# Down-weight sums moved two quads earlier, and the last activations stored in four pieces, in a macaron decoder layer in float32

## The chip, the cores and the metric

The kernel runs on one core of a Trainium2 chip. The time is device microseconds of one execution; the median of several runs is compared. The engines are named as in the profile: PE (TensorE), ACT (ScalarE), DVE (VectorE), POOL (GpSimd) and SP (SyncE, which here only issues DMAs and waits).

## The reference

```python
def swiglu(h, w_gu, w_down):
    g, u = jnp.split(h @ w_gu, 2, axis=-1)
    return (jax.nn.silu(g) * u) @ w_down
...
x = x + 0.5 * swiglu(rms_norm(x, ffn1_norm), ffn1_w_gu, ffn1_w_down)
h = rms_norm(x, mix_norm)
# q, k, v, u = split(h @ w_in): sliding-window attention beside causal pooling
x = x + concat([a, m]) @ w_out
x = x + 0.5 * swiglu(rms_norm(x, ffn2_norm), ffn2_w_gu, ffn2_w_down)
gate = sigmoid(rms_norm(x, ple_norm) @ ple_w_gate + ple_b_gate)
x = x + gate * rms_norm(p @ ple_w_proj, ple_post_norm)
```

Sequence 1024, model width 1024, hidden width 2816, all float32. The change touches the two `swiglu` calls only.

## The kernel before

Everything lies transposed (channels on partitions, tokens on the free axis). Each float32 factor is split into a high part (ACT rounds it to float32r) and a low part (DVE subtracts), and a product is three matmuls: high x high, low x high, high x low (helper `three`, lines 779 to 781). A matmul is 128 x 128 by 128 x 512.

Both matrix products of a feed-forward are computed as 2 x 2 blocks with seven block products instead of eight (P1, P2, Q3 to Q7), which needs sums and differences of the operands' blocks.

**Gate-and-up stage.** 22 quads, q = 0 to 21. A quad is one pair of hidden tiles; it loads 1 MB of weights (`quad_load`, into `raw[q % 2]`), DVE and ACT form and split its seven sums a quad ahead (`add_t`, `round_t`, `split_t`), and PE makes seven products of 12 matmuls each. DVE then gates the quad (`gated`), and behind every odd quad it forms the sums of the activations (`mix_acts`). SP stores these seven tiles of 128 x 512, 1792 KB, to DRAM as `actc[ph, j]`, j = 0 to 10 (`act_store`); the buffer `acts` is then free for the next pair.

**Down stage.** 77 steps: seven products in the order `ORDER2` = P1, P2, Q6, Q5, Q3, Q7, Q4, each over k = 0 to 10 (`FH` is 11). A step takes one tile `actc[ph, k][:, s, :]` and one block of down weights, both 256 KB, loads them into one of six ring slots (`ring_load`, `d_f`), ACT rounds the slot (`dn_hi`, line 1139), DVE subtracts (`dn_lo`, line 1620), and PE runs 12 matmuls on it. Slot i is loaded again when PE has done step i - 6. P1, P2 and Q3 read weights as given (`wd`), the others read sums of weights (`wdc`).

**The sums of the down weights** are made during the gate-and-up stage, in 22 chunks of 512 KB: SP loads a chunk into the single buffer `wdr` (`wd_load`, which waits until the chunk before is stored), POOL makes four additions in place (line 738), SP stores it (`wd_store`, which waits for POOL). They are first read by step 22.

**SP's order is written by hand** (`ffn` in the SP block), and every wait in it blocks all that stands behind. Turn q, from 1 to 21: in even turns the store of the activations of the pair before; load of chunk q - 1; its store; the gate-up load of quad q + 3 (waits for the split of quad q + 1). In turn 21 the ring loads of steps 0 to 3 stand ahead of chunk 20's load, and step 4's ring load ahead of its store. Then: load of chunk 21, ring load of step 5, store of chunk 21, ring load of step 6, store of the last activations (pair 10, one DMA of 1792 KB), ring load of step 7, and so on. From step 12 on each ring load is followed by a reload of a tile of x into memory that the activations used, so SP waits there once for all their stores.

`ph` is 0 for the first feed-forward and 1 for the second. ACT works strictly in program order too: behind step 12's rounding it copies the four P1 banks (`dp`), on which PE's step 11 and the rest of P2 depend.

Of the kernel before, what the change touches and what calls it, by code (L numbers as in the profile page):

```python
# [40 lines left out]
FH = FT // 2  # L41
# [32 lines left out]
P1, P2, Q6, Q7, Q5, Q4, Q3 = range(7)  # L74
# [5 lines left out]
QUADS = FT  # L80
# [13 lines left out]
RING = 6  # L94
STEP_INC = FH + 3

EARLY = 3
WD_AT = {P1: 0, P2: 2, Q3: 3}
WDC_AT = {Q5: 0, Q7: 1, Q4: 2, Q6: 3}
N_WD = 2 * FH  # L100

RES_FFN = 2 * KT
RES_MIX = 2 * KT
# [133 lines left out]
def program(nc, xT, pT, units, gu, wd, poolw, small, const, onehot, rel, band, e_dram, actc, wdc, x1, out):  # L237
    with ExitStack() as ctx:
# [7 lines left out]
        def place(name, shape, at, dt=F32):  # L246

            assert base <= at and at + size_of(shape) <= limit, (name, at, limit)
            return nc.alloc_sbuf_tensor_at(name, list(shape), dt, offset=at)
# [22 lines left out]
        def block_at(k, a):  # L272
            return r0 + 4 * KB * k + 2 * KB * a
# [5 lines left out]
        acts = place("acts", (P, 8, HALF), block_at(4, 0))  # L279
# [132 lines left out]
        def sem(name):  # L412
            return ctx.enter_context(nc.semaphore(name))
# [26 lines left out]
        gu_made, p1_copied, g0_made, g1_made = sem("gu_made"), sem("p1_copied"), sem("g0_made"), sem("g1_made")  # L440
        w2_made, w3_made, c22_made, c21_made, c12_made = (sem(n) for n in ("w2_made", "w3_made", "c22_made", "c21_made", "c12_made"))
        act_made, act_mixed, act_out = sem("act_made"), sem("act_mixed"), sem("act_out")
        wd_in, wd_made, wd_out = sem("wd_in"), sem("wd_made"), sem("wd_out")
        s2_in, t2_in = [sem(f"s2_in{i}") for i in range(RING)], [sem(f"t2_in{i}") for i in range(RING)]
        dn_rounded, dn_split, dn_made, dp_made = sem("dn_rounded"), sem("dn_split"), sem("dn_made"), sem("dp_made")
# [39 lines left out]
        def t_count(ph, n):  # L485

            return ph * (NGU - FIRST) + n + (1 if ph else 1 - FIRST)

        def t_ready(ph, n):
            return (t_pool, n + 1) if ph == 0 and n < FIRST else (t_split, t_count(ph, n))  # L490
# [7 lines left out]
        def step_done(ph, i):  # L498
            return dn_count(ph, i // FH, i % FH)
# [34 lines left out]
        def _(sp):  # L534
# [9 lines left out]
            def quad_load(ph, q):  # L544
                sp.dma_start(raw[q % 2][:, :], gu[ph, q]).then_inc(gu_in[q % 2], 16)

            def wd_load(ph, c):
                if c:
                    sp.wait_ge(wd_out, 16 * (ph * N_WD + c))
                else:  # L550
                    sp.wait_ge(s_made, (ph + 1) * N_MADE)
                sp.dma_start(wdr[:, :, 0:HALF], wd[ph, c // 2, c % 2].rearrange("p (i b) n -> p i (b n)", b=2)).then_inc(wd_in, 16)

            def wd_store(ph, c):
                sp.wait_ge(wd_made, 4 * (ph * N_WD + c + 1))
                sp.dma_start(wdc[ph, c // 2, c % 2].rearrange("p (i b) n -> p i (b n)", b=2), wdr[:, :, 0:HALF]).then_inc(wd_out, 16)

            def act_store(ph, j):
                sp.wait_ge(act_mixed, 4 * (ph * FH + j + 1))
                sp.dma_start(actc[ph, j], acts[:, 0:PRODUCTS, :]).then_inc(act_out, 16)  # L560

            def ring_load(ph, i):
                s, k, slot = ORDER2[i // FH], i % FH, i % RING
                if i >= RING:
                    sp.wait_ge(dn_made, step_done(ph, i - RING))
                elif i < 2:
                    sp.wait_ge(t_split, t_count(ph, GU_AT[(QUADS - 2 + i, Q3)]))
                else:
                    sp.wait_ge(gu_made, ph * NGU + NGU - 12 + 2 * (i - 1))
                if s == P1:  # L570
                    sp.wait_ge(act_out, 16 * (ph * FH + k + 1))
                elif s in WDC_AT:
                    sp.wait_ge(wd_out, 16 * (ph + 1) * N_WD)
                weights = wd[ph, k][:, :, WD_AT[s], :] if s in WD_AT else wdc[ph, k][:, :, WDC_AT[s], :]
                sp.dma_start(d_f[slot][:, 0:HALF], actc[ph, k][:, s, :]).then_inc(s2_in[slot], 16)
                sp.dma_start(d_f[slot][:, HALF:2 * HALF].rearrange("p (h n) -> p h n", h=2),
                             weights.rearrange("h p n -> p h n")).then_inc(t2_in[slot], 16)

            def x_reload(ph, n):
                a, k = n // KT, n % KT  # L580
                src = xT if ph == 0 else x1
                sp.dma_start(x_sb[:, k, tok(a)], src[k * P:(k + 1) * P, tok(a)]).then_inc(x_back[n // KH], 16)

            def ffn(ph, first_units):
                for q in (0, 1):
                    done, value = t_ready(ph, GU_AT[(q, Q3)])
                    sp.wait_ge(done, value)
                    quad_load(ph, q + 2)
                for q in range(1, QUADS):
                    if q == QUADS - 1:  # L590

                        for i in range(4):
                            ring_load(ph, i)
                    if q % 2 == 0:
                        act_store(ph, q // 2 - 1)
                    wd_load(ph, q - 1)
                    if q == QUADS - 1:
                        ring_load(ph, 4)
                    wd_store(ph, q - 1)
                    if q + 3 < QUADS:  # L600
                        sp.wait_ge(t_split, t_count(ph, GU_AT[(q + 1, Q3)]))
                        quad_load(ph, q + 3)
                wd_load(ph, N_WD - 1)
                ring_load(ph, 5)
                wd_store(ph, N_WD - 1)
                for i in range(RING, STEPS):
                    if i == RING + 1:
                        act_store(ph, FH - 1)
                    if i == FH + 1:
                        sp.wait_ge(wd_out, 16 * (ph + 1) * N_WD)  # L610
                        sp.wait_ge(act_out, 16 * (ph + 1) * FH)
                        sp.wait_ge(act_made, (ph + 1) * 2 * QUADS)
                    ring_load(ph, i)
                    if FH < i <= FH + 2 * KT:
                        x_reload(ph, i - FH - 1)
                    if i >= FH + 4 and (i - FH - 4) % 4 == 0 and first_units:
                        if len(first_units) >= SLOTS:
                            sp.wait_ge(gu_made, (ph + 1) * NGU)
                        unit_load(first_units.pop(0))
                    if i == 4 * FH:  # L620
                        sp.wait_ge(x_step, ph * XS + 3 * KH)
                        if ph == 0:
                            skewed = bass.AP(tensor=band.tensor, offset=P - 1,
                                             ap=[[SKEW - 1, P], [P * SKEW, N_Q_HEADS], [1, 2 * P]])
                            sp.wait_ge(band_out, 16 * N_Q_HEADS)
                            sp.dma_start(bias[:, :, :], skewed).then_inc(bias_in, 16)
                        else:
                            for j in range(4):
                                sp.wait_ge(e_out[j], 16 * (2 * KT // 4))
                            for a in (0, 1):  # L630
                                sp.wait_ge(re_out[a], 16)
                            sp.wait_ge(act_made, 4 * QUADS)
                            sp.dma_start(re_sb[0][:, :], e_dram[0, :, KT, :]).then_inc(re_in[0], 16)
                    if ph == 1 and 4 * FH < i <= 4 * FH + KT:
                        d = i - 4 * FH - 1
                        sp.dma_start(e_sb[0][:, d, :], e_dram[0, :, d, :]).then_inc(e_in[0], 16)
# [741 lines left out]
        def _(dve):  # L1378
# [131 lines left out]
            def gated(ph, q):  # L1510

                b, i, odd = ph * QUADS + q, q % 2, q % 2
                if not odd and b >= 2:
                    dve.wait_ge(act_out, 16 * (b // 2))
                dve.wait_ge(c12_made, b + 1)
                dve.wait_ge(g0_made, b + 1)
                dve.tensor_tensor(acts[:, (P1, P2)[odd], :], g0[i][:, :], w2[i][:, :], ALU.mult).then_inc(act_made, 1)
                dve.wait_ge(g1_made, b + 1)
                dve.tensor_tensor(acts[:, (A21, Q4)[odd], :], w3[i][:, :], c22[i][:, :], ALU.mult).then_inc(act_made, 1)
# [255 lines left out]
            for step in PLAN:  # L1775
# [16 lines left out]
                elif kind == "qks":  # L1792
                    a, what, i = step[1:]
                    j = QKS_AT[step[1:]]
# [5 lines left out]
                elif kind == "scores":  # L1800
# [3 lines left out]
                    for h in range(HPK):  # L1804

                        c = (h % 2) * 2 * P
# [6 lines left out]
                    c = C_SINK + kv * HPK  # L1813
# [14 lines left out]
                elif kind == "pv":  # L1828
                    u = step[1]
                    b, p0 = u // 2, (u % 2) * HEAD_DIM  # L1830
# [143 lines left out]
```

## Time and profile before

| | us |
|---|---|
| median of 3 timed runs | 1786.76 (1786.72 to 1788.21) |
| the profiled execution, whole | 1789.44 |
| its span, first to last instruction | 1787.3 |
| PE busy (matmul) | 1704.6, 95% |
| DVE busy | 1296.6, 73% |
| ACT busy | 697.2, 39% |
| POOL busy | 302.2, 17% |
| mean granted TensorE clock | 0.976 of full speed |

The mean rate of the DMAs over the span is 155 GB/s. The chain that ended last runs through PE for 72% of the span and DVE for 16%.

How to read the rows further down: a timeline row gives the start in microseconds from the start of the span, the duration, the engine, the line, the operation, what it writes and reads, how many instructions are merged in it, and in brackets how long the engine sat idle before it and what ended that. SPq rows are DMAs being issued; their duration is that of the issue. The first down stage begins (PE) at 507 us and the second at 1472 us.

### The profile page before, as it was taken

What the parts mean: (1) busy time and instruction counts of PE and PEld (TensorE: products, weight loads), DVE (VectorE), ACT (ScalarE), POOL (GpSimd) and SP (SyncE); (2) the same over time, 40 slices, a digit from 0 to 9 for tenths busy, and PEclk for the clock granted to TensorE, in tenths of its full rate; (3) what the DMA queues carried; (4) which work ended last, traced back from release to release, by engine and by line L of the source; (5) the groups of instructions that cost most, each with busy time, mean ns of one, the idle gap of its engine ahead of it and who ended that gap; (6) DMA issues with size and microseconds to landing.
All of it is one profiled execution on the core that took longest, in us unless ns stands there. A gap on an engine that the chain in (4) does not pass through costs nothing.

```text
span 1787.3 us, 20459 instructions
## 1 busy us (share of the span) xinstructions
PE 1704.6 (95%) x7314; PEld 1377.8 (77%) x7314; DVE 1296.6 (73%) x1812; ACT 697.2 (39%) x1120; POOL 302.2 (17%) x292
## 2 busy tenths in 40 slices
PE   7589999999999999999999889999999999999998
PEld 4368888888878887767677768888888887888877
DVE  7988677677655758678778699767767754676786
ACT  5343233232235444345645443322323323534442
POOL 5801222111220000024231001211122211000000
PEclk9789999999999999999899989999999999999999
DMA  7215444444469766121122313444444447876433
GB/s 283 75 49 212 153 165 148 159 166 158 139 232 312 218 212 199 48 71 48 36 77 81 114 71 120 175 159 154 170 155 164 147 151 269 289 235 204 153 117 125
DMA packets 124144, 277.69 MB, mean 155 GB/s; under 512 B 10219, under 2 KB 51852, under 8 KB 115468
## 3 DMA queue, kind: packets, MB, share of 16 engines
q1 hardware_dynamic: 116748, 263.02, 43.5%
q10 hardware_dynamic: 7296, 13.37, 2.1%
q8 instruction: 59, 0.97, 0.2%
q14 instruction: 41, 0.34, 0.1%
HBM read 198.23 MB, written 78.12 MB: 155 GB/s over the span
## 4 chain that ended last, share of the span: by engine, by line
PE 72%; DVE 16%; ACT 4%; DMA 3%; issue 3%; POOL 1%; SPq 1%; ACTq 0%; DVEq 0%; POOLq 0%
PE bank L779 23%; PE bank L780 23%; PE bank L781 23%; DVE qb L1796 1%; PE bank L1001 1%; DVE acc L1393 1%; DVE x_sb L1425 1%; DVE w_lo L1628 1%; DVE h_lo L1437 1%; DMA wdr<-in_wd 1%; DMA d_f<-in_wd 1%; ACT probs L1329 1%; DVE hn L1405 1%; DVE probs L1808 1%; POOL wdr L738 1%
## 5 line engine op out<-in xcount | busy, mean ns | idle before, releaser
L738 POOL TENSOR_TENSOR wdr<-wdr 128x256 f32<-128x256 f32 x176 | 172.1, 978 | 783.7 <-DMA wdr<-in_wd 773.4
L1620 DVE TENSOR_TENSOR dn_lo<-d_f,dn_hi 128x1024 fp32r<-128x1024 f32 x154 | 191.0, 1255 | 130.5 <-ACT dn_hi L1139 129.9
L779 PE MATMUL bank<-h_hi,t_hi 128*128 128x512 f32 x704 | 278.1, 395 | 6.4 <-DVE h_lo L1437 6.4
L780 PE MATMUL bank<-h_lo,t_hi 128*128 128x512 f32 x704 | 275.3, 391 | 0.0
L781 PE MATMUL bank<-h_hi,t_lo 128*128 128x512 f32 x704 | 275.2, 391 | 0.0
L779 PE MATMUL bank<-dn_hi 128*128 128x512 f32 x616 | 243.1, 395 | 9.4 <-DVE dn_lo L1620 9.4
L780 PE MATMUL bank<-dn_lo,dn_hi 128*128 128x512 f32 x616 | 241.8, 392 | 0.0
L781 PE MATMUL bank<-dn_hi,dn_lo 128*128 128x512 f32 x616 | 241.7, 392 | 0.0
L1139 ACT ACTIVATE dn_hi<-d_f 128x1024 fp32r<-128x1024 f32 x154 | 161.0, 1058 | 172.6 <-DMA d_f<-in_wd 102.9
L779 PE MATMUL bank<-c_hi,t_hi 128*128 128x512 f32 x528 | 205.5, 389 | 0.7 <-DVE c L1496 0.7
L781 PE MATMUL bank<-c_hi,t_lo 128*128 128x512 f32 x528 | 205.4, 389 | 0.0
L780 PE MATMUL bank<-c_lo,t_hi 128*128 128x512 f32 x528 | 205.4, 389 | 0.0
L779 PE MATMUL bank<-h_hi,w_hi 128*128 128x512 f32 x416 | 172.7, 415 | 7.4 <-ACT sig L1369 2.6
L780 PE MATMUL bank<-h_lo,w_hi 128*128 128x512 f32 x416 | 164.0, 394 | 0.0
L781 PE MATMUL bank<-h_hi,w_lo 128*128 128x512 f32 x416 | 163.6, 393 | 0.0
L779 PEld LDWEIGHTS bank<-h_hi,t_hi 128*128 128x128 f32 x704 | 133.3, 189 | 37.3 <-DVE h_lo L1437 5.2
L780 PEld LDWEIGHTS bank<-h_lo,t_hi 128*128 128x128 f32 x704 | 133.3, 189 | 28.8 <-issue 1.2
L781 PEld LDWEIGHTS bank<-h_hi,t_lo 128*128 128x128 f32 x704 | 133.0, 189 | 27.7
L1113 ACT ACTIVATE t_hi<-t_f 128x512 fp32r<-128x512 f32 x168 | 100.5, 624 | 126.4 <-DVE t_f L1457 119.1
L779 PEld LDWEIGHTS bank<-dn_hi 128*128 128x128 f32 x616 | 116.8, 190 | 37.2 <-DVE dn_lo L1620 12.3
L781 PEld LDWEIGHTS bank<-dn_hi,dn_lo 128*128 128x128 f32 x616 | 116.8, 190 | 24.6
L780 PEld LDWEIGHTS bank<-dn_lo,dn_hi 128*128 128x128 f32 x616 | 116.8, 190 | 24.5 <-issue 0.5
(165 smaller groups left out, 2607.0 us busy)
## 6 DMA issues: line engine op xcount, KB each, us to landing
raw<-in_gu SPq DMA_DIRECT2D x44, 1024.0 KB, 5.7
actc<-acts SPq DMA_DIRECT2D x22, 1792.0 KB, 6.7
d_f<-actc SPq DMA_DIRECT2D x154, 256.0 KB, 3.4
raw_m<-in_units SPq DMA_DIRECT2D x52, 512.0 KB, 4.1
wdr<-in_wd SPq DMA_DIRECT2D x44, 512.0 KB, 6.0
wdc<-wdr SPq DMA_DIRECT2D x44, 512.0 KB, 3.4
d_f<-wdc SPq DMA_DIRECT2D x88, 256.0 KB, 3.2
d_f<-in_wd SPq DMA_DIRECT2D x66, 256.0 KB, 4.7
```

The lines of the kernel that those rows point to most:

```text
L738: pool.tensor_tensor(blocks[to], blocks[one], blocks[two], ALU.add).then_inc(wd_made, 1)
L779: pe.matmul(ps, whi, vhi, start=first, stop=False, skip_group_check=onto)
L780: pe.matmul(ps, whi, vlo, start=False, stop=False, skip_group_check=onto)
L781: return pe.matmul(ps, wlo, vhi, start=False, stop=last, skip_group_check=onto)
L1001: last = pe.matmul(score_bank[h // 2][:, c + off:c + 2 * P], q_sb[p0:p0 + HEAD_DIM, h, b * P:(b + 1) * P], k_sb[p0:p0 + HEAD_DIM, max(b - ...
L1113: act.activation(t_hi[i][:, :], src, ACT.Copy).then_inc(t_rounded, 1)
L1139: act.activation(dn_hi[slot][:, :], d_f[slot][:, :], ACT.Copy).then_inc(dn_rounded, 1)
L1329: last = act.activation(probs[:, h, off:], probs[:, h, off:], ACT.Exp, bias=stats[:, NEGM, h:h + 1], accum_out=stats[:, DEN, h:h + 1])
L1393: dve.tensor_tensor(a, a, sq[i % 2][:, :], ALU.add).then_inc(squares_added, 1)
L1405: dve.scalar_tensor_tensor(hn[k % 2][:, :], x_sb[:, k, tok(nrm % 2)], col(g), rstd[nrm % 2][:, :], ALU.mult, ALU.mult).then_inc(h_normed, 1)
L1425: dve.scalar_tensor_tensor(x, x, col(C_GAIN[2 * ph] + k), rstd[a][:, :], ALU.mult, ALU.mult).then_inc(s_made, 1)
L1620: dve.tensor_tensor(dn_lo[slot][:, :], d_f[slot][:, :], plain(dn_hi[slot][:, :]), ALU.subtract).then_inc(dn_split, 1)
```

## The change

`WD_TURN` gives each of SP's turns its chunks: one a turn, but two in turns 6, 10 and 14, so that chunk 20 falls in turn 18, chunk 21 in turn 19, and none in turns 20 and 21. A chunk is now loaded and stored without anything in between (`wd_chunk`). The last activations are stored in four DMAs, `LAST` = slots 0, 1 to 2, 3 to 4 and 5 to 6 of the seven (256, 512, 512, 512 KB), each with a semaphore of its own, ahead of the ring loads of steps 7, 8, 9 and 10. A ring load with k = 10 waits for its piece. DVE's gating in the second feed-forward waits, in even quads, for all four pieces of the first.

```diff
+LAST = [(0, 1), (1, 3), (3, 5), (5, 7)]
...
+WD_TWO = (6, 10, 14)
+WD_TURN, _at = {}, 0
+for _q in range(1, QUADS):
+    _n = min(2 if _q in WD_TWO else 1, N_WD - _at)
+    WD_TURN[_q] = tuple(range(_at, _at + _n))
+    _at += _n
...
+            def last_store(ph, i):
+
+                lo, hi = LAST[i]
+                sp.wait_ge(act_mixed, 4 * (ph + 1) * FH)
+                sp.dma_start(actc[ph, FH - 1][:, lo:hi, :], acts[:, lo:hi, :]).then_inc(last_out[i], 16)
+
+            def wd_chunk(ph, c):
+                wd_load(ph, c)
+                wd_store(ph, c)
...
             def ring_load(ph, i):
...
-                if s == P1:
-                    sp.wait_ge(act_out, 16 * (ph * FH + k + 1))
-                elif s in WDC_AT:
+                if k == FH - 1:
+                    piece = [j for j, (lo, hi) in enumerate(LAST) if lo <= s < hi][0]
+                    sp.wait_ge(last_out[piece], 16 * (ph + 1))
+                elif s == P1:
+                    sp.wait_ge(act_out, 16 * (ph * (FH - 1) + k + 1))
+                if s in WDC_AT:
                     sp.wait_ge(wd_out, 16 * (ph + 1) * N_WD)
...
-                    wd_load(ph, q - 1)
+                    for c in WD_TURN.get(q, ()):
+                        wd_chunk(ph, c)
                     if q == QUADS - 1:
                         ring_load(ph, 4)
-                    wd_store(ph, q - 1)
...
-                wd_load(ph, N_WD - 1)
                 ring_load(ph, 5)
-                wd_store(ph, N_WD - 1)
                 for i in range(RING, STEPS):
-                    if i == RING + 1:
-                        act_store(ph, FH - 1)
+                    if RING + 1 <= i <= RING + len(LAST):
+                        last_store(ph, i - RING - 1)
                     if i == FH + 1:
                         sp.wait_ge(wd_out, 16 * (ph + 1) * N_WD)
-                        sp.wait_ge(act_out, 16 * (ph + 1) * FH)
+                        for j in range(len(LAST)):
+                            sp.wait_ge(last_out[j], 16 * (ph + 1))
...
                 if not odd and b >= 2:
-                    dve.wait_ge(act_out, 16 * (b // 2))
+                    dve.wait_ge(act_out, 16 * (b // 2 - ph))
+                    if ph:
+                        for j in range(len(LAST)):
+                            dve.wait_ge(last_out[j], 16)
```

## Rows read from the trace of the kernel before

**Rows 1.** Busy us of each engine (instructions) by stretch, granted clock, DMA share, GB/s.

```profile
510.00:540.00 30.00, 25.62 (x105) 20.40 (x104) 16.29 (x14) 8.49 (x8) 5.53 (x4) 0.94 0.73 254
...
1060.00:1440.00 380.00, 378.27 (x1656) 312.42 (x1655) 283.60 (x423) 121.21 (x213) 72.73 (x76) 0.99 0.43 152
1470.00:1500.00 30.00, 25.61 (x102) 20.35 (x101) 14.01 (x15) 8.44 (x9) 5.31 (x4) 0.92 0.68 241
```

**Rows 2.** PE's waits, 520 to 560 and 1480 to 1520: total us, times, longest.

```profile
PE bank L779 <- DVE dn_lo L1620: 4.4, 2, 3.6
...
PE bank L779 <- DVE dn_lo L1620: 4.4, 2, 2.6
```

**Rows 3.** Timeline of PE where both down stages begin.

```profile
518.29 0.39 PE L779 MATMUL bank<-dn_hi 128*128 128x512 f32 x1
...
521.01 0.39 PE L779 MATMUL bank<-dn_hi 128*128 128x512 f32 x1
...
531.29 0.50 PE L779 MATMUL bank<-dn_hi 128*128 128x512 f32 x1 [3.57 <-DVE dn_lo L1620]
...
533.05 0.63 PE L779 MATMUL bank<-dn_hi 128*128 128x512 f32 x1
...
538.49 0.39 PE L779 MATMUL bank<-dn_hi 128*128 128x512 f32 x1
...
1485.76 0.39 PE L779 MATMUL bank<-dn_hi 128*128 128x512 f32 x1
...
1504.84 0.39 PE L779 MATMUL bank<-dn_hi 128*128 128x512 f32 x1
```

**Rows 4.** Timeline of ACT in the first down stage: steps 6, 7, 9, 10.

```profile
522.32 1.06 ACT L1139 ACTIVATE dn_hi<-d_f 128x1024 fp32r<-128x1024 f32 x1 [9.12 <-DMA d_f<-in_wd]
528.92 1.06 ACT L1139 ACTIVATE dn_hi<-d_f 128x1024 fp32r<-128x1024 f32 x1 [5.53 <-DMA d_f<-in_wd]
...
532.59 1.06 ACT L1139 ACTIVATE dn_hi<-d_f 128x1024 fp32r<-128x1024 f32 x1 [0.36 <-DMA d_f<-in_wd]
534.02 1.06 ACT L1139 ACTIVATE dn_hi<-d_f 128x1024 fp32r<-128x1024 f32 x1 [0.37 <-DMA d_f<-in_wd]
```

**Rows 5.** Timeline of SP's queue around the start of the first down stage.

```profile
503.57 0.56 SPq L556 DMA_DIRECT2D wdc<-wdr  x1
506.66 0.58 SPq L552 DMA_DIRECT2D wdr<-in_wd  x1
...
517.34 0.55 SPq L575 DMA_DIRECT2D d_f<-actc  x1
...
518.82 0.55 SPq L560 DMA_DIRECT2D actc<-acts  x1
```

**Rows 6.** Timeline of DVE: the last pair of activations is mixed.

```profile
509.66 3.04 DVE L1528 TENSOR_TENSOR acts<-acts 128x512 f32<-128x512 f32 x4
```

**Rows 7.** DMA issues: count, KB each, median us from issue to landing.

```profile
raw<-in_gu SPq DMA_DIRECT2D x44, 1024.0 KB, 5.7
actc<-acts SPq DMA_DIRECT2D x22, 1792.0 KB, 6.7
```

**Rows 8.** Busy us by stretch, as in rows 1, while the old store runs.

```profile
520.00:525.00 5.00, 4.19 (x19) 3.18 (x18) 1.23 (x1) 1.06 (x1) 0.00 (x0) 1.00 1.10 413
```

**Rows 9.** Timeline of SP's queue in quads 6 and 7.

```profile
220.33 0.61 SPq L545 DMA_DIRECT2D raw<-in_gu  x1
223.10 0.57 SPq L552 DMA_DIRECT2D wdr<-in_wd  x1
231.87 0.54 SPq L556 DMA_DIRECT2D wdc<-wdr  x1
```

**Rows 10.** Timeline of ACT: first reading of quad 9's weights.

```profile
244.26 0.62 ACT L1113 ACTIVATE t_hi<-raw 128x512 fp32r<-128x512 f32 x1
```

**Rows 11.** Timeline of DVE: the sum and the gating of an even quad (8).

```profile
260.09 0.69 DVE L1508 TENSOR_TENSOR w<-bank,w 128x512 f32<-128x512 f32 x1 [2.03 <-PE bank L781]
260.87 0.69 DVE L1517 TENSOR_TENSOR acts<-g,w 128x512 f32<-128x512 f32 x1
```

More of the change, by code:

```diff
@@ L98 @@
 WD_AT = {P1: 0, P2: 2, Q3: 3}
+LAST = [(0, 1), (1, 3), (3, 5), (5, 7)]
 WDC_AT = {Q5: 0, Q7: 1, Q4: 2, Q6: 3}
 N_WD = 2 * FH
+WD_TWO = (6, 10, 14)
[4 more added lines that the diff above has]
+    _at += _n
+assert _at == N_WD
 RES_FFN = 2 * KT
@@ L442, in program @@
         act_made, act_mixed, act_out = sem("act_made"), sem("act_mixed"), sem("act_out")
+        last_out = [sem(f"last_out{i}") for i in range(len(LAST))]
         wd_in, wd_made, wd_out = sem("wd_in"), sem("wd_made"), sem("wd_out")
```

## Prediction

> **What bounds the kernel now.** I read the stretches first. They show TensorE (PE) busy for 378.27 of 380 us in the gate-and-up stage, but only 25.6 of 30 us where each of the two down stages begins, and there the granted clock falls to 0.94 and 0.92 [rows 1]. So PE is the bound, the gate-up stage has almost nothing left, and the holes lie at the two seams. The waits say what ended them: both times PE waited 4.4 us in two waits for dn_lo, VectorE's (DVE's) split of a ring slot [rows 2].
>
> The PE timeline sizes the holes. A step of the down stage is 12 matmuls, and takes 521.01 - 518.29 = 2.72 us. In the first down stage step 5 begins at 521.01 and step 9 at 538.49: four steps took 17.48 us where 10.88 is regular, so 6.60 us are lost. In the second they ran from 1485.76 to 1504.84, 19.08 us, so 8.20 us are lost [rows 3]. Together that is 14.80 us: 8.8 us of idle time [rows 2], and 6.0 us because PE runs at the lower clock level (1.2 GHz; matmuls of 0.63 us instead of 0.39) for some 8 matmuls behind a gap [rows 3]. From step 9 on a step is 2.72 us again.
>
> Then I asked who is late. PE waits for DVE, DVE for ScalarE (ACT), and ACT sat idle for 9.12 us ahead of step 6 and 5.53 us ahead of step 7 until the DMA into the ring slot landed [rows 4]. Why these DMAs were late stands in SP's queue [rows 5]. The slot of step 6 was free when PE ended step 0, at 521.01 - 4 x 2.72 = 510.13. But SP had the store of the second-last sums at 503.57, the last down-weight load at 506.66, and then had to wait until POOL had made the last sums and to store them; only then came the load of step 6, at 517.34, 7.2 us late. Behind it went the store of the last activations, 1792 KB in one DMA, at 518.82, and the load of step 7 was queued behind that: its slot had been free at 512.85, its data reached ACT at 528.92, 9 us after its issue. The second down stage has the same order of events.
>
> **The change, part by part.**
>
> Sums two quads sooner. The 22 chunks (load, four POOL adds, store) are all there still, but 20 and 21 move to quads 18 and 19, because quads 6, 10 and 14 take two. Between quad 20's activation store and step 6's load nothing of them is left. Step 6's load now follows its own gate at 510.2. With 4 to 5 us to land (my estimate from its old 517.34 to ACT at 522.32 [rows 4, 5]) and 2.4 us for ACT and DVE (528.92 for the ACT start, 531.29 for the PE start [rows 3, 4]) it is ready by about 517.6. PE wants it at 507.41 + 6 x 2.72 = 523.73: 6 us to spare. This takes away step 6's wait.
>
> The last activations in four pieces (256, 512, 512, 512 KB). The mix of the last pair ends at 509.66 + 3.04 = 512.70 [rows 6]. SP is then about to issue step 7's load (slot free at 512.85), so piece 0 goes at about 512.8, and pieces 1, 2, 3 behind the loads of steps 7, 8, 9, at about 514, 516.5 and 519.3. Bytes on the queue from 512.8 up to and with step 10's load (issued at 521.3): 1792 + 4 x 512 = 3840 KB, 3.93 MB. PE wants step 10 at 507.41 + 27.2 = 534.6; less 2.4 us for ACT and DVE and some 2 us from last byte to ACT, they must have moved by 530.2. That needs 3.93 MB in 17.4 us, 226 GB/s. What the queue can do: 1792 KB in 6.7 us, 274 GB/s, when one store runs alone [rows 7]; 413 GB/s in the 5 us window in which the old store and two loads overlapped [rows 8]; and between steps 9 and 10 ACT starts 1.43 us apart, 512 KB each, 367 GB/s [rows 4]. I take the higher figures, as they are for a full queue like this one; step 10 is then ready at about 528 with 6 us to spare. At 274 GB/s it is ready at about 531.5, and still no wait. So steps 6 to 12 all keep a margin. The thinnest is at step 12: ACT must round its slot before it copies the P1 banks that PE's step 11 builds on, and SP, ahead of that load, waits for all four pieces. At 274 GB/s piece 3 has landed at about 527, the load goes out then rather than at 526.5 and ACT has it at about 533; the copies are due from 535.4. It holds, by about 2 us.
>
> Here a rule of the notes speaks against the change. A full queue moved 413 GB/s, with DMAs of 256 to 1792 KB on it [rows 8]. The Trainium skill, page "DMA: Bandwidth & Descriptors", section "Rules for kernel authors", wants at least 1 MiB in a DMA for full bandwidth, and its section on the anatomy of a DMA gives each about 2.0 us of fixed time; three more DMAs would then cost up to 6 us a stage, if none of it overlapped. The rows have the overlap, so in my sum it is 0; as a rival it is below, priced by rows.
>
> Both gaps gone, PE has no pause between 507 and 545, and the trace shows matmuls of 0.63 us only behind gaps [rows 3]; so the 6.0 us of low clock go too. What is late next? Nothing within reach: the steps that still lose a little later in the stage (the norm's sum, and ACT in the last eleven steps) sit on ACT's order and keep their cost.
>
> Two chunks in quads 6, 10 and 14. In quad 6 SP stored its one chunk and issued quad 9's gate-up load at 220.33. Now that load stands behind a second chunk. As the next chunk was loaded at 223.10 and stored at 231.87 anyway, the second one keeps these times, and quad 9's load goes out at about 232.5, 12.1 us later [rows 9]. A gate-up load takes 5.7 us [rows 7]: landed at about 238.2, or 241 beside other traffic. ACT first reads it at 244.26 [rows 10], 3 to 6 us later. That rounding comes right behind the first of the running quad's seven products, so PE begins quad 9 some 6 x 2.72 = 16.3 us later, and a load that is late would first eat that too. Then quad 7's chunk moves behind it (load 235.2, store about 245), quad 10's load goes out at about 245.6, due one quad (7 x 2.72 = 19.0 us) after 244.26, at 263.3; quad 8's activation store slips by under 1 us, and by quad 9 the queue is where it was. Cost 0; if the cover failed, 6 places (three a phase) would pay. POOL's adds beside DVE's work are as many as before.
>
> Waits. In phase 1 DVE waits for four more semaphores in each of 11 even quads, ahead of the gating, with the mixes and the next quad's adds queued behind. From the end of L1508 (260.09 + 0.69) to the start of L1517 (260.87) is 0.09 us with three waits in it [rows 11]; four more that have long been met are at most 0.12 us, and DVE sits idle for 2.03 us just ahead of them [rows 11]. Cost 0, bounds 0 and 11 x 0.12 = 1.3 us. SP issues six more DMAs in all: 0.5 us each, in a queue that now waits for PE's steps.
>
> **Sum.** 1787.3 (span) - 14.8 = 1772.5 us; with the 2.14 us around the span the profiled execution was 1789.44, so a profiled run of the new kernel would be near 1774.6. That profiled run was 2.7 us over the median of the three timed ones, 1786.76. From the median: 1786.76 - 14.80 = 1771.96. Own bounds: below, the sum and the 1.7 us that gate-up still loses (380 - 378.27 [rows 1]), should SP's other order help there, 1770.2; above, 1.3 us for the waits and one small wait per stage of about 1 us, 1775.3.
>
> **The rivals.**
> (a) The pieces go through the queue one behind the other, each with its own latency: 3.09 us for 512 KB, as the lone store of sums took before the next load (503.57 to 506.66 [rows 5]). Then 3840 KB are 7.5 x 3.09 = 23.2 us from 512.8, step 10 would be ready at 536.0 + 2.4 = 538.4, 3.8 us late, in each stage, some of it at low clock again: 1771.96 + 2 x 3.8 = 1779.6, with a microsecond or two more for the clock. For it: the rule above. Against: the 1.43 us and the 413 GB/s. I give it 0.12.
> (b) The change doesn't do what it says: something else than SP's order holds step 6 or 7, so that most of the loss comes back (1783 to 1787). Against it: SP's gates read from the code and the PE times leave 6 us. 0.03.
> (c) The other side. SP's double chunks let the gate-up loads of quads 9, 13 and 17 come too late. Mechanism: ACT waits for raw, DVE's adds wait, PE runs out of split tiles. It decides only from a load that lands 3 to 6 us after my time plus the 16.3 us by which ACT's first rounding leads PE: a load of some 25 us where 5.7 is usual. To end slower by more than 0.2% (3.6 us) it must eat 14.8 + 3.6 = 18.4 us in 6 places, 3.1 us each: 1790.4. 0.02.
> (d) The forecast, 0.83.
>
> **How the numbers follow.** About 0.2% (3.6 us) is what a measurement of this kernel can tell from no change. Faster: all of (d), all of (a), half of (b): 0.96. Same: the other half of (b) and a mild (c), 0.025. Slower 0.015. The range takes the forecast's own bounds, 1770.2 to 1775.3, widened by about 0.5 us at either end for the scatter of the timed runs and on the upper side a little into (a): 1769.8 to 1776.8.
>
> **What would show it.** In SP's queue: no down-weight DMA behind quad 19; step 6's load near 510.2 and step 7's near 513; four stores of activations between loads, each later load issued 2.72 us behind the last. PE: no wait for dn_lo around steps 5 to 9, no matmul of 0.63 us there, first step of the down stage to step 9 in 24.5 us, clock 1.00. ACT: no idle of 9 us. Gate-up: quad 9's load at about 232.5, PE as dense as before. I am wrong if steps 10 to 12 wait for DMA (then the queue's rate was mis-sized), if the waits by quads 9, 13, 17 appear, or if the slow matmuls stay without a gap.

## Result and profile after

| | before | after |
|---|---|---|
| median, us | 1786.72 (5 runs, 1779.89 to 1788.21) | 1770.14 (5 runs, 1768.02 to 1770.47) |
| ratio | | 0.9913, 95% interval 0.9893 to 0.9932 |
| profiled execution; its span | 1789.44; 1787.3 | 1770.31; 1768.2 |
| PE busy | 1704.6 | 1697.4 |

The kernel is 0.9% faster. The forecast was 1772.0 us, from 1769.8 to 1776.8.

Lines of the changed file are shifted: 802 to 804 are the old 779 to 781 (PE), 1162 the old 1139 (ACT's rounding of a slot), 577 the stores of the pieces, 571 the other activation stores, 599 and 600 the two ring loads, 563 and 567 load and store of a chunk of sums, 556 the gate-up load, 1136 the old 1113 (ACT's rounding of gate-up weights), 1646 the old 1620 (DVE's split of a slot), 761 the old 738 (POOL's additions). In the kernels of the experiments they are shifted by a few lines more.

The stretches first, after (columns as in [rows 1]; behind the length of the stretch stand the busy times of PE, of PE's weight loads, of DVE, ACT and POOL, then the granted clock, the DMA share and GB/s):

```profile
510.00:540.00 30.00, 30.00 (x134) 24.86 (x133) 15.04 (x15) 12.35 (x14) 0.00 (x0) 1.00 0.90 286
1050.00:1430.00 380.00, 378.35 (x1656) 312.96 (x1657) 284.29 (x422) 121.33 (x214) 78.88 (x88) 0.99 0.45 161
1460.00:1490.00 30.00, 30.00 (x134) 24.85 (x133) 16.47 (x17) 11.03 (x12) 0.00 (x0) 1.00 0.76 243
```

Where [rows 1] had 25.6 busy microseconds of 30 and clocks of 0.94 and 0.92, PE is now busy for all 30 at 1.00, at both seams. The gate-up stage is as full as it was: 378.35 of 380 against 378.27. POOL has nothing left to do at the seams.

SP's queue at the first seam, after (start us, duration us, engine, line, operation; compare [rows 5]):

```profile
460.67 0.54 SPq L567 DMA_DIRECT2D wdc<-wdr  x1
473.57 0.33 SPq L571 DMA_DIRECT2D actc<-acts  x1
474.03 0.36 SPq L599 DMA_DIRECT2D d_f<-actc  x1
...
509.66 0.32 SPq L599 DMA_DIRECT2D d_f<-actc  x1
510.02 0.44 SPq L600 DMA_DIRECT2D d_f<-in_wd  x1
511.65 0.32 SPq L577 DMA_DIRECT2D actc<-acts  x1
512.38 0.32 SPq L599 DMA_DIRECT2D d_f<-actc  x1
512.74 0.46 SPq L600 DMA_DIRECT2D d_f<-in_wd  x1
513.25 0.47 SPq L577 DMA_DIRECT2D actc<-acts  x1
515.10 0.32 SPq L599 DMA_DIRECT2D d_f<-actc  x1
```

The last sums are stored at 460.67. Step 6's load goes out at 509.66, where its slot becomes free; in [rows 5] it was 517.34. Step 7's follows 2.72 us later, with one piece of 256 KB between, and from there the loads keep PE's pace.

ACT, steps 6 to 12, after (in brackets the idle time before and what ended it; compare [rows 4]):

```profile
513.25 1.06 ACT L1162 ACTIVATE dn_hi<-d_f 128x1024 fp32r<-128x1024 f32 x1 [4.82 <-DMA d_f<-in_wd]
516.42 1.06 ACT L1162 ACTIVATE dn_hi<-d_f 128x1024 fp32r<-128x1024 f32 x1 [2.11 <-DMA d_f<-in_wd]
519.84 1.06 ACT L1162 ACTIVATE dn_hi<-d_f 128x1024 fp32r<-128x1024 f32 x1 [2.35 <-DMA d_f<-in_wd]
522.67 1.06 ACT L1162 ACTIVATE dn_hi<-d_f 128x1024 fp32r<-128x1024 f32 x1 [1.77 <-DMA d_f<-in_wd]
526.57 1.06 ACT L1162 ACTIVATE dn_hi<-d_f 128x1024 fp32r<-128x1024 f32 x1 [2.84 <-DMA d_f<-in_wd]
528.00 1.06 ACT L1162 ACTIVATE dn_hi<-d_f 128x1024 fp32r<-128x1024 f32 x1 [0.38 <-DMA d_f<-in_wd]
530.64 1.06 ACT L1162 ACTIVATE dn_hi<-d_f 128x1024 fp32r<-128x1024 f32 x1 [1.58 <-DMA d_f<-in_wd]
```

ACT still waits for DMA at every step, but now that costs nothing: PE starts its down stage at 506.75 and wants step 10 at 533.95, and ACT has it at 526.57. A wait of an engine that is ahead is no loss; in [rows 4] the same kind of bracket was one.

### The profile page after: what moved, and what is told of

Its sections match the earlier page's. It is cut to its first block, busy times and chain, and to the rows that moved or that the text cites. A ratio compares the mean times of both kernels' runs of the same rounds, so it can differ in the third digit from the quotient of the medians.

```text
span 1768.2 us, 20493 instructions
## 1 busy us (share of the span) xinstructions
PE 1697.4 (96%) x7314; PEld 1374.6 (78%) x7314; DVE 1291.0 (73%) x1812; ACT 695.4 (39%) x1120; POOL 288.2 (16%) x292
## 4 chain that ended last, share of the span: by engine, by line
PE 76%; DVE 16%; ACT 4%; issue 3%; DMA 1%; SPq 0%; ACTq 0%; DVEq 0%
PE bank L802 25%; PE bank L803 25%; PE bank L804 25%; DVE qb L1822 1%; DVE hn L1428 1%; PE bank L1024 1%; ACT probs L1352 1%; DVE w_lo L1654 1%; DVE x_sb L1448 1%; DVE rstd L1421 1%; DVE probs L1834 1%; DVE h_lo L1460 1%; DVE dn_lo L1646 1%; DVE probs L1847 1%; DVE h_lo L1434 1%
## 5 line engine op out<-in xcount | busy, mean ns | idle before, releaser
L1646 DVE TENSOR_TENSOR dn_lo<-d_f,dn_hi 128x1024 fp32r<-128x1024 f32 x154 | 185.8, 1222 | 119.1 <-ACT dn_hi L1162 118.8
L761 POOL TENSOR_TENSOR wdr<-wdr 128x256 f32<-128x256 f32 x176 | 158.4, 900 | 685.9 <-DMA wdr<-in_wd 675.5
```

The costliest lines, as they stand in the source:

```text
L761: pool.tensor_tensor(blocks[to], blocks[one], blocks[two], ALU.add).then_inc(wd_made, 1)
L1646: dve.tensor_tensor(dn_lo[slot][:, :], d_f[slot][:, :], plain(dn_hi[slot][:, :]), ALU.subtract).then_inc(dn_split, 1)
```

## Where the time went

PE executes the same 7314 matmuls in both kernels, so its timeline can be laid side by side and cut where the stages begin. Worked out from PE's start times in five profiles of the kernel before (the first and four more, below) and three of the changed one; "loss" is the time from step 5 to step 9 less 10.88 us, as in the prediction:

| us | loss, first seam | loss, second seam | both down stages | between them | span |
|---|---|---|---|---|---|
| before, 1 | 6.60 | 8.20 | 437.1 | 746.8 | 1787.3 |
| before, 2 | 2.68 | 6.02 | 431.0 | 742.2 | 1776.5 |
| before, 3 | 2.01 | 8.26 | 432.7 | 745.3 | 1781.0 |
| before, 4 | 6.98 | 8.38 | 437.8 | 741.7 | 1783.3 |
| before, 5 | 7.47 | 8.14 | 438.1 | 742.8 | 1783.9 |
| after, 1 | 0 | 0 | 422.3 | 743.1 | 1768.2 |
| after, 2 | 0 | 0 | 422.3 | 741.2 | 1766.5 |
| after, 3 | 0 | 0 | 422.3 | 741.8 | 1767.9 |

The mean span falls from 1782.4 to 1767.5, by 14.9 us. 13.0 of these lie in the down stages, and the loss at the seams (13.0 on average) is all of them. Nearly all of the rest, 1.7 us, lies between the two down stages (attention, pooling, the second gate-up stage), which took 741.7 to 746.8 us in the kernel before and 741.2 to 743.1 in the changed one.

## Experiments

Each run was made beside runs of the kernel before on the same chip. In the first series, of four kernels, the kernel before had a median of 1784.46 us (11 runs), in the second 1786.35 (8 runs).

**The changed kernel again.**

> The changed kernel once more, as the yardstick of this chip. Both down stages without a gap at steps 5 to 8. The stretch between the two feed-forwards (attention and pooling), which was 3.8 us shorter in its first profile than in that of the kernel before, tells whether that came by chance: theory A says it moves by a few us from run to run in either kernel; the rival says that the change shortens it and it is short again in all the kernels of this call.

1768.61 us (1768.54 to 1769.88), ratio 0.9911 (0.9896 to 0.9926); no loss at either seam. The stretch between was 741.2 us, 1.9 us shorter than in its first profile, so it moves by itself by that much; whether the change shortens it is taken up below.

**One part alone: the sums early, the store whole.**

```diff
-                    if RING + 1 <= i <= RING + len(LAST):
-                        last_store(ph, i - RING - 1)
+                    if i == RING + 1:
+                        act_store(ph, FH - 1)
```

(The semaphores of the pieces go with it; this is the kernel before with `WD_TURN`.)

> One part alone: the down-weight sums two quads sooner, but the last activations still stored in one DMA of 1792 KB ahead of step 7's ring load. Theory A (SP's order is the whole cause, the queue is fast enough): step 6's load goes out at its gate (near 510), the store near 512, step 7's load right behind it, at ACT some 9 us later as before, near 522, ready near 524, and PE wants it near 526. No wait, no slow matmul; the time is that of the changed kernel, 1770 to 1772 us, 16 us under the kernel before. Theory B (the four pieces are needed): step 7 still waits, 1 to 3 us in each stage with slow matmuls behind it, 1774 to 1778 us.

1770.06 us, ratio 0.9919 (0.9906 to 0.9933); PE's stretch from step 5 to step 9 has no loss at either seam. SP and ACT of this kernel at the first seam:

```profile
510.13 0.32 SPq L583 DMA_DIRECT2D d_f<-actc  x1
510.49 0.44 SPq L584 DMA_DIRECT2D d_f<-in_wd  x1
512.13 0.32 SPq L568 DMA_DIRECT2D actc<-acts  x1
512.85 0.32 SPq L583 DMA_DIRECT2D d_f<-actc  x1
513.21 1.21 SPq L584 DMA_DIRECT2D d_f<-in_wd  x1
```

```profile
521.60 1.06 ACT L1146 ACTIVATE dn_hi<-d_f 128x1024 fp32r<-128x1024 f32 x1 [6.75 <-DMA d_f<-in_wd]
```

Step 7's load still takes 8.4 us to ACT behind 1792 KB (9.0 in [rows 4]), and it still arrives: DVE is done at 523.92, PE wants the slot at 526.26. With the pieces that margin is 7.0 us instead of 2.3. So theory A holds, and the four pieces buy margin and no time that can be seen. Of 1770.06 against 1768.61 us the down stages hold nothing, as they take the same time to 0.1 us in both kernels, and the runs of the two overlap (1769.32 to 1771.20, and 1768.54 to 1769.88).

**The other part alone: the pieces, the sums where they were.**

```diff
-                    for c in WD_TURN.get(q, ()):
-                        wd_chunk(ph, c)
+                    wd_load(ph, q - 1)
                     if q == QUADS - 1:
                         ring_load(ph, 4)
+                    wd_store(ph, q - 1)
...
+                wd_load(ph, N_WD - 1)
                 ring_load(ph, 5)
+                wd_store(ph, N_WD - 1)
```

> The other part alone: the last activations in four pieces, the sums where they were. Theory A: step 6's load is as late as before (near 517), so the first gap stays (0.8 us in the first stage, 2.6 us in the second, with slow matmuls behind it), but step 7's load has only 256 KB ahead of it and arrives in time, so the second gap (3.6 and 1.8 us) goes. Of 14.8 us some 8 to 10 come back: 1777 to 1780 us. Theory B (both parts are needed, each of them alone gives little): within 3 us of the kernel before.

1777.71 us, ratio 0.9958 (0.9942 to 0.9973): 6.8 us under the kernel before. The loss at the seams is 3.48 and 4.25 us. PE's rows with a gap of over 0.2 us at the first seam and at the second:

```profile
526.37 0.50 PE L804 MATMUL bank<-dn_hi 128*128 128x512 f32 x1 [2.12 <-DVE dn_lo L1648]
529.65 0.50 PE L804 MATMUL bank<-dn_hi 128*128 128x512 f32 x1 [0.26 <-DVE dn_lo L1648]
535.72 0.50 PE L804 MATMUL bank<-dn_hi 128*128 128x512 f32 x1 [0.34 <-DVE dn_lo L1648]
...
1483.11 0.50 PE L804 MATMUL bank<-dn_hi 128*128 128x512 f32 x1 [2.36 <-DVE dn_lo L1648]
```

Step 6's gap stays, as expected, and of the gap of 3.57 us ahead of step 7 [rows 3] 0.26 is left; step 9 waits for 0.34 us too. Both loads still stand behind the same wait for POOL: step 7's went out at 521.35, with its slot free since 513.20, and reached ACT at 527.28. The time lies in the range of theory A, but less came back than its 8 to 10 us: 6.8 us of time, and 5.2 of the 13.0 us that the seams lose on average. The parts do not add: sums early takes away all, pieces alone somewhat under half.

**Is it the sums' traffic, or SP's waiting?** The last sums are loaded as late as before and the store is whole, but SP no longer waits for POOL's last additions ahead of the ring loads of steps 6, 7 and 8. It waits for them behind step 8's load, by when they are done. (The wait for the second-last sums still stands ahead of step 6's load, and is over 6 us before that load may go.)

```diff
-                    wd_store(ph, q - 1)
+                    if q < QUADS - 1:
+                        wd_store(ph, q - 1)
...
-                wd_load(ph, N_WD - 1)
                 ring_load(ph, 5)
-                wd_store(ph, N_WD - 1)
+                wd_store(ph, N_WD - 2)
+                wd_load(ph, N_WD - 1)
...
+                    if i == RING + 3:
+                        wd_store(ph, N_WD - 1)
```

> The sums stay in their old turns and the store stays one DMA, but SP no longer waits for POOL ahead of a ring load: chunk 20 is stored behind step 5's load, chunk 21 is stored behind step 8's load. If it is SP's blocking order that costs, step 6's load goes out at its gate (near 510) and the time is that of the changed kernel within 2 us (1770 to 1773). If it is the traffic of the sums at the seam that costs, step 7 or 8 waits again, and the time is 4 us or more above it.

1770.89 us, ratio 0.9922 (0.9908 to 0.9936), no loss at the seams. SP's queue of this kernel:

```profile
503.83 0.56 SPq L556 DMA_DIRECT2D wdc<-wdr  x1
506.93 0.58 SPq L552 DMA_DIRECT2D wdr<-in_wd  x1
510.19 0.33 SPq L575 DMA_DIRECT2D d_f<-actc  x1
...
512.60 0.33 SPq L560 DMA_DIRECT2D actc<-acts  x1
...
517.29 0.55 SPq L556 DMA_DIRECT2D wdc<-wdr  x1
```

Chunk 20 is stored and chunk 21 loaded within 0.3 us of their times in [rows 5], chunk 21 is stored 0.6 us later than in the first profile of the kernel before (517.29 against 516.68), and step 6's load goes out at its gate all the same. All the traffic of the kernel before is at the seam, and the whole gain is there. The cause is the one wait for POOL, with the store behind it, ahead of step 6's ring load; moving the sums is one way to be rid of it. The margin at step 7 is the smallest of the three kernels without a loss so far, 1.9 us.

**The price of small DMAs.** Seven pieces of 256 KB back to back ahead of step 7's load:

```diff
-LAST = [(0, 1), (1, 3), (3, 5), (5, 7)]
+LAST = [(i, i + 1) for i in range(7)]
...
-                    if RING + 1 <= i <= RING + len(LAST):
-                        last_store(ph, i - RING - 1)
+                    if i == RING + 1:
+                        for j in range(len(LAST)):
+                            last_store(ph, j)
```

> The price of small DMAs by itself. The changed kernel, but the last activations go out in seven DMAs of 256 KB, back to back, ahead of step 7's load, where the run with one store of 1792 KB had the same bytes in the same place and step 7's slot ready 2.3 and 2.7 us before PE wanted it. Theory A (DMAs overlap on the queue): only SP's seven issues of 0.5 us count; step 7's load goes out 1 to 4 us later, its slot is ready 0 to 2 us before PE wants it; 1769 to 1772 us. Theory B (each DMA pays its own latency, 3 us for 512 KB or 2 to 3 us for 256 KB): 14 to 20 us from the first piece to the last, step 7 waits 6 us or more in each stage, 1782 us or more.

1769.77 us, ratio 0.9907 (0.989 to 0.9923). SP and ACT at the first seam:

```profile
511.76 4.00 SPq L577 DMA_DIRECT2D actc<-acts  x7
515.86 0.59 SPq L599 DMA_DIRECT2D d_f<-actc  x1
```

```profile
521.50 1.06 ACT L1163 ACTIVATE dn_hi<-d_f 128x1024 fp32r<-128x1024 f32 x1 [7.08 <-DMA d_f<-in_wd]
```

SP spends 4.0 us on issuing, so step 7's load goes out 3 us later than with one store, and its data reaches ACT at 521.50 against 521.60: the same. Seven small DMAs and one large one, with ring loads beside them, moved the same bytes in the same time, and step 7 was ready 2.1 us before PE wanted it. Had each of the seven paid 2 to 3 us of its own, one behind the other, step 7 would have waited 6 us or more. Rival (a) falls.

**How much may a gate-up load be late?** Three chunks in turn 6 and four in turn 12:

```diff
-WD_TWO = (6, 10, 14)
+WD_MANY = {6: 3, 12: 4}
...
-    _n = min(2 if _q in WD_TWO else 1, N_WD - _at)
+    _n = min(WD_MANY.get(_q, 1), N_WD - _at)
```

> The changed kernel, but with three chunks of sums in turn 6 and four in turn 12 instead of two in turns 6, 10 and 14. Each chunk too many delays the gate-up load behind it by 11 to 12 us. Quad 9's load (turn 6) goes out near 242 and lands near 248, some 5 us after ACT's usual first reading; quad 15's load (turn 12) goes out near 368, lands near 374, some 16 us after it. Theory A (as I forecast: ACT's lead of 16 us over PE is cover too): nothing at turn 6, 0 to 5 us at turn 12 in each feed-forward: 1769 to 1780 us. Theory B (DVE's additions of a quad stand in its queue ahead of the sums that free PE's banks, so PE stops soon after ACT and DVE wait): 2 to 5 us at turn 6 and 10 to 16 us at turn 12 in each feed-forward: 1793 to 1812 us.

1793.12 us, ratio 1.0043 (1.0027 to 1.0058): slower than before, though its seams are free of loss. Theory B holds for turn 12 and theory A for turn 6. SP, ACT, DVE and PE of this kernel, for quad 15's load:

```profile
365.79 0.54 SPq L567 DMA_DIRECT2D wdc<-wdr  x1
366.38 0.61 SPq L556 DMA_DIRECT2D raw<-in_gu  x1
```

```profile
372.38 0.63 ACT L1136 ACTIVATE t_hi<-raw 128x512 fp32r<-128x512 f32 x1 [14.13 <-DMA raw<-in_gu]
```

```profile
372.39 0.69 DVE L1480 TENSOR_TENSOR t_f<-raw 128x512 f32<-128x512 f32 x1 [12.78 <-DMA raw<-in_gu]
...
379.10 0.68 DVE L1519 TENSOR_TENSOR c<-bank,w 128x512 f32<-128x512 f32 x1
```

```profile
370.83 0.39 PE L804 MATMUL bank<-c_hi,t_lo 128*128 128x512 f32 x1
379.93 0.77 PE L802 MATMUL bank<-c_hi,t_hi 128*128 128x512 f32 x1 [8.71 <-DVE c L1519]
380.49 0.63 PE L803 MATMUL bank<-c_lo,t_hi 128*128 128x512 f32 x1
```

PE does not stop for the weights of quad 15, which it needs much later. It stops for `make_c22` of the quad that runs (old line 1496), which frees the bank for its Q3 product and which stands in DVE's queue behind additions and splits for quad 15. DVE sat idle for 12.8 us, and PE lost 8.7 us and some 2.9 us more, most of it in matmuls at 1.2 GHz; laid beside the changed kernel, PE comes out of this turn 11.6 us later, and 11.5 us later out of the same turn of the second feed-forward. So the cover behind DVE's wait is about 12.8 - 8.7 = 4 us. At turn 6, with three chunks, ACT waited for the load:

```profile
248.72 0.63 ACT L1136 ACTIVATE t_hi<-raw 128x512 fp32r<-128x512 f32 x1 [4.70 <-DMA raw<-in_gu]
```

DVE sat idle for 3.4 us, and PE had all of its 20 us between 240 and 260, so this was within the cover. In the changed kernel quad 9's load goes out at 230.83 and lands at 236.5, and ACT reads it at 243.60 and DVE at 244.98, neither with a wait. With three chunks it landed at 248.6, 12.1 us later, and cost nothing.

**Why the kernel before scatters.** Its timed runs spread over 9 us, those of the changed kernel over 3.

> The kernel before once more, for its profile. Its timed runs scatter over 9 us (1779.9 to 1788.7), those of the changed kernel over 3. Theory A: the scatter sits in the seams themselves (how many matmuls run at the low clock behind the two gaps, and how long each gap is): the loss at steps 5 to 8, 6.6 and 8.2 us in the first profile, differs by some us, while the stretch between the feed-forwards stays within 2 us. Theory B: the scatter sits in attention and pooling, where the first profile was 3.7 us longer than that of the changed kernel: that stretch (746.6 us from the end of the first down stage to the start of the second) differs by 3 us or more and the seams agree within 1 us.

The spans were 1776.5 us here and 1781.0 in the run beside it, which had the same expectation. The loss at the two seams together differs by up to 6.1 us among these three profiles (table above), and the stretch between by 4.6: both theories hold in part. At the first seam of this run (busy times of the stretch, then PE's only wait there):

```profile
505.00:535.00 30.00, 27.64 (x122) 22.39 (x121) 17.47 (x17) 10.65 (x11) 4.46 (x4) 1.00 0.76 263
```

```profile
528.87 0.50 PE L779 MATMUL bank<-dn_hi 128*128 128x512 f32 x1 [2.36 <-DVE dn_lo L1620]
529.21 0.40 PE L780 MATMUL bank<-dn_lo,dn_hi 128*128 128x512 f32 x1
```

Step 6 was in time by 1.2 us, so there was one gap of 2.36 us ahead of step 7, and the clock stayed at 1.00. In the first profile there were two gaps, 0.81 and 3.57 us, and matmuls at 1.2 GHz behind the second. The first seam thus costs 2 to 3 us or about 7, and it goes with the time at which POOL is done: SP stored the last sums at 514.22 here and at 516.68 in the first profile. All ten seams of the five profiles agree. Counted from PE's start of the stage, that store went out at 6.3 and 7.0 us where the loss was 2.0 and 2.7 us, at 9.3 us three times (6.6 to 7.5 us lost) and at 10.8 us five times (6.0 to 8.4 us lost).

Which gap brings the low clock does not follow from its length, and what decides it no run here shows. In the run with the pieces alone the second stage had a single gap of 2.36 us as well, and there seven matmuls of 0.63 us came behind it, of which this is the first:

```profile
1483.96 0.63 PE L804 MATMUL bank<-dn_hi 128*128 128x512 f32 x1
```

> The stretch from the end of the first down stage to the start of the second took 746.8, 742.2 and 745.3 us in three profiles of the kernel before, and 741.2 to 743.5 in five kernels without a gap at the seams. If a gap at the first seam makes it longer, this profile has it at 744 us or more as well; if it is chance, it falls anywhere from 741 to 747, and the loss at the two seams, 8.7 to 14.8 us so far, with it.

The stretch was 741.7 us here and 742.8 in the run beside it (spans 1783.3 and 1783.9), with the largest losses at the first seam of all. A gap at the seam need not lengthen what follows. The 3.7 us by which this stretch was shorter in the first profile of the changed kernel are thus best taken as chance, but that is not shown: the two longest, 746.8 and 745.3 us, are both of the kernel before, and none of the seven profiles of the changed kernel and of the experiments has over 743.5 (the one with many chunks left out, as it loses time in this stretch). A third profile of the changed kernel, taken with these, had a time of 1770.02 us, a span of 1767.9 and 741.8 in the stretch.

## Why the prediction was right, point by point

**What bounds.** Right: two holes at the seams. The down stages gained 13.0 us, and the loss at the seams is all of it.

**Sums two quads sooner.** Right in place and size. Step 6's load was forecast for 510.2 and went out at 509.66; its slot was to be ready at 517.6 and was at 516.16, 6.9 us before PE wanted it (forecast 6).

**The last activations in four pieces.** The load of step 10 was to be ready at about 528 and was at 528.88, with 5.1 us to spare (forecast 6); the queue moved 356 GB/s between 515 and 520 us and 317 in the next 5 us, somewhat less than the 367 to 413 that I took. Step 12, the thinnest in the forecast, was with ACT at 530.64, ahead of the copies due from 535.4. What the text left out is that these pieces were not needed: it named the store of 1792 KB as what made step 7 late, and did not ask whether it still would be once step 6's load and the store itself went out 5 to 7 us sooner. Sums early alone gave the whole gain. As both parts were made, the sum was not wrong by it, only the credit.

**Low clock.** Right in that no matmul at 1.2 GHz is left at the seams, and the 6.0 us went with the gaps. But these 6.0 us were only what was left of the loss after the idle time, and the low clock is not all of it. At the first seam 7 matmuls of 0.63 us stand behind the second gap and none behind the first, at the second seam there are 14. Each is 0.43 us from the next instead of 0.23, which makes 4.2 us. The rest is matmuls that the slow stretch covers in part, the restart behind each gap (0.34 us to the next matmul, as from 531.29 to 531.63), and idle time that the profile counts only from a matmul's modelled end. The sum is the same, as all of it hangs on the gaps.

**The size, 14.8 us.** It was one draw, and that it came so close is in part luck. In five profiles of the kernel before the loss is 8.7 to 15.6 us, 13.0 on average; the mean spans differ by 14.9 us, the timed medians by 16.6 and, in the series of experiments, 15.9. The median came out 1.9 us under my number. The profiled run came out 4.3 us under its own (1770.31 against 1774.6), and 3.7 us of that are the shorter stretch between the down stages. I had one profile and put no scatter of the loss into the range. With the 8.7 us of the second profile the same sum would have given 1778.1 us, outside of it.

**Two chunks in quads 6, 10 and 14.** Cost 0, as forecast. Quad 9's load was forecast for 232.5 (went out at 230.83) and quad 10's for 245.6 (241.75).

**Rival (c): the step that was wrong.** I gave the gate-up load the 16.3 us by which ACT's rounding leads PE as cover, and had PE stop only for want of split tiles. The run with many chunks shows about 4 us behind DVE's wait: the additions of the next quad stand in DVE's queue ahead of a sum of the running quad. DVE first reads quad 9's weights at 244.98 in the changed kernel. With 4 us more the load must land by about 249, which is 18 us after it goes out, where I had some 25, and 12 to 13 us after it lands now. The changed kernel stays clear of that, but by little over one chunk: a third chunk in turn 6 was still free (landed at 248.6), a fourth in turn 12 cost about 11.5 us per feed-forward.

**Waits of DVE.** No cost to be seen: the gate-up stretch of the second feed-forward is as full as before.

**What stays open.** The timed medians differ by 1 to 2 us more than the mean profiled spans, and the stretch between the down stages by 1.7 us in the mean. No run here tells whether either is scatter.

## What to carry to other kernels

An engine that only issues DMAs is a queue too: a wait for a slow helper (here POOL, for sums that nobody needs for another 40 us) must not stand ahead of a load that the bound engine needs next, and re-ordering one wait can be worth as much as moving the work. To find how late a transfer may be, follow the consumer's whole queue and not only the data's own user: what is stuck behind the waiting instruction can be needed much sooner. And when two edits are made together, ask of each what it still does once the other is in.

## What the runs showed of the hardware

First, what had not been in my sum: POOL's four additions of a chunk take 3.2 to 5.8 us, and DVE pays too. In the first profile of the kernel before, the last chunk, one addition while DVE was idle and one while it worked all through, and DVE's splits of three slots beside it:

```profile
510.89 5.76 POOL L738 TENSOR_TENSOR wdr<-wdr 128x256 f32<-128x256 f32 x4 [7.34 <-DMA wdr<-in_wd]
...
498.45 0.74 POOL L738 TENSOR_TENSOR wdr<-wdr 128x256 f32<-128x256 f32 x1 [12.17 <-DMA wdr<-in_wd]
...
513.38 1.60 POOL L738 TENSOR_TENSOR wdr<-wdr 128x256 f32<-128x256 f32 x1
...
512.63 5.11 DVE L1620 TENSOR_TENSOR dn_lo<-d_f,dn_hi 128x1024 fp32r<-128x1024 f32 x3
```

A chunk and the splits of four slots in the changed kernel:

```profile
237.95 3.19 POOL L761 TENSOR_TENSOR wdr<-wdr 128x256 f32<-128x256 f32 x4 [7.73 <-DMA wdr<-in_wd]
...
511.54 4.62 DVE L1646 TENSOR_TENSOR dn_lo<-d_f,dn_hi 128x1024 fp32r<-128x1024 f32 x4
```

Beside POOL, DVE split ring slots at 1.68 us a slot; without POOL, in the changed kernel, at 1.14 us. The Trainium skill, page "SBUF — State Buffer", section "Who interferes with whom", says that a DVE instruction with two inputs in SBUF contends with a GpSimd instruction that reads SBUF. Both are of that kind here, and the trace agrees. So the wait that held step 6's load was itself longer for what DVE mixed and split at the same time, by an estimate of 2.6 us (5.76 less 3.19).

Second, what my sum had taken from two rows of the kernel before: a queue that is full moves as much in seven pieces of 256 KB as in one of 1792 KB (521.50 against 521.60 us). The rule of at least 1 MiB in the Trainium skill, page "DMA: Bandwidth & Descriptors", section "Rules for kernel authors", does not decide here. The fixed 2.0 us of a DMA, which the prediction took from that page's section on the anatomy of a DMA, is given there for DMAs that GpSimd issues. In this kernel SP issues them, and the run shows no such time per piece, only 0.57 us of SP's own for each issue (4.00 us for seven).
